# A two-layer hybrid encoder on one core: loads in turn, rotary angles beside the gated unit, first step sizes on GpSimd, one wait fewer at the recurrence

## The reference, cut to what matters

```python
proj = x @ w_in[i]
# recurrence: dt = exp(log_dt); lam_bar = exp(lam * dt); scan; gelu; gated unit
lam_bar = jnp.exp(lam * dt)
y = jax.nn.gelu(y.reshape(bsz, L, W_A))
y = y * jax.nn.sigmoid(y @ w_glu.astype(f32) + b_glu.astype(f32))
# attention: rotary angles of the positions, the same in both layers
ang = pos.astype(jnp.float32)[:, :, None, None] * inv
cos, sin = jnp.cos(ang), jnp.sin(ang)
...
mixed = jnp.sum(gates * lifted, axis=2) @ w_out[i]
x = layer_norm(DEEPNORM_ALPHA * x + mixed + ple, ln_g[i], ln_b[i])
```

## Time and profile before

| | us |
|---|---|
| median of three runs | 2646.0 |
| lowest, highest | 2645.92, 2646.96 |
| span of the profiled execution (first to last instruction) | 2645.0 |
| PE busy | 2577.1 |
| DVE busy | 1861.1 |
| ACT busy | 1288.8 |
| POOL busy | 111.0 |

### The profile page before, as it was taken

One profiled execution on the slowest core, in us unless ns is written; L12 is line 12 of the kernel. 1 busy time (PEld: TensorE's weight loads), 2 busy tenths in 40 slices (PEclk: granted clock), 3 DMA queues, 4 the chain that ended last, 5 costly groups with the idle time before them and its releaser, 6 DMA issues.

```text
span 2645.0 us, 41799 instructions
## 1 busy us (share of the span) xinstructions
PE 2577.1 (97%) x13736; PEld 2151.2 (81%) x13736; DVE 1861.1 (70%) x3251; ACT 1288.8 (49%) x2334; POOL 111.0 (4%) x206
## 2 busy tenths in 40 slices
PE   6999999999999999999989999999999999999998
PEld 5888999977777778898778999989767777788986
DVE  7788877834777776556678877887357777765666
ACT  5555555543444334443465555555334443444535
POOL 2100000000000000000021000000000000000000
PEclk9999999999999999999999999999999999999999
DMA  7544444434444335555464444444344444355454
GB/s 245 173 143 148 154 147 148 151 120 143 151 155 164 126 110 177 186 174 174 160 202 154 154 148 148 146 153 149 116 151 152 165 132 134 119 182 190 168 175 143
DMA packets 115956, 411.83 MB, mean 156 GB/s; under 512 B 15460, under 2 KB 15514, under 8 KB 115584
## 3 DMA queue, kind: packets, MB, share of 16 engines
q1 hardware_dynamic: 107424, 391.17, 43.9%
q0 software_dynamic: 8416, 19.18, 2.3%
HBM read 403.99 MB, written 6.29 MB: 155 GB/s over the span
## 4 chain that ended last, share of the span: by engine, by line
PE 93%; DVE 3%; issue 2%; ACT 2%; DMA 1%; PEldq 0%; PEld 0%; DVEq 0%; POOL 0%; POOLq 0%; ACTq 0%
PE bank L1623 29%; PE bank L1663 20%; PE bank L1665 10%; PE bank L2003 7%; PE bank L1580 5%; PE bank L1598 4%; PE bank L1753 2%; PE bank L1735 2%; PE bank L1923 2%; PE bank L1716 2%; PE bank L1937 1%; PE bank L1701 1%; PE bank L1821 1%; PE bank L1903 1%; PE bank L1845 1%
## 5 line engine op out<-in xcount | busy, mean ns | idle before, releaser
L384 ACT ACTIVATE WH<-ring 128x512 fp32r<-128x512 f32 x1364 | 854.8, 631 | 1136.5 <-PE bank L1623 473.0
L398 DVE TENSOR_TENSOR WL<-ring,WH 128x512 fp32r<-128x512 f32 x852 | 572.9, 688 | 417.6 <-ACT WH L384 415.2
L1663 PE MATMUL bank<-XX,WH 128*128 128x512 f32 x2304 | 823.7, 401 | 27.7 <-DVE XX L567 15.8
L1665 PE MATMUL bank<-XX,WL 128*128 128x256 f32 x2304 | 645.5, 280 | 0.0
L1663 PEld LDWEIGHTS bank<-XX,WH 128*128 128x128 f32 x2304 | 436.5, 189 | 130.1 <-DVE XX L567 15.8
L1623 PE MATMUL bank<-WH,XX 128*128 128x512 f32 x1536 | 485.2, 397 | 4.5 <-issue 3.5
L389 DVE TENSOR_TENSOR WL<-ring,WH 128x512 fp32r<-128x512 f32 x512 | 350.7, 688 | 140.1 <-ACT WH L384 135.9
L1665 PEld LDWEIGHTS bank<-XX,WL 128*128 128x128 f32 x2304 | 438.2, 190 | 0.0
L1623 PEld LDWEIGHTS bank<-WH,XX 128*128 128x128 f32 x1536 | 284.9, 188 | 81.4 <-issue 22.3
L1623 PE MATMUL bank<-WL,XX 128*128 128x512 f32 x768 | 299.9, 390 | 0.0
L1580 PE MATMUL bank<-ARENA,ring 128*128 128x256 f32 x704 | 158.3, 387 | 13.5 <-ACT ARENA L1368 11.0
(11 more groups left out here) (311 smaller groups left out, 3329.2 us busy)
## 6 DMA issues: line engine op xcount, KB each, us to landing
ring<-in_blocks SPq DMA_DIRECT2D x738, 512.0 KB, 3.3
ARENA<-in_bc POOLq DMA_DIRECT2D x2, 2048.0 KB, 8.9
ARENA<-in_decay POOLq DMA_DIRECT2D x8, 512.0 KB, 4.1
ARENA<-in_x SPq DMA_DIRECT2D x4, 512.0 KB, 9.3
u_scratch<-ARENA POOLq DMA_DIRECT2D x16, 128.0 KB, 2.4
ARENA<-u_scratch POOLq DMA_DIRECT2D x64, 32.0 KB, 3.1
y_scratch<-ARENA POOLq DMA_DIRECT2D x16, 128.0 KB, 2.0
ARENA<-y_scratch POOLq DMA_DIRECT2D x64, 32.0 KB, 2.7
```

Of the source, the lines that this page charges most:

```text
L384: nc.scalar.activation(wh[q], raw(which[0], q), ACT.Copy).then_inc(wh_ready[q], 1)
L398: vec.tensor_tensor(wl[q], raw(which[0], q), wh[q].bitcast(F32), ALU.subtract).then_inc(w_used[slot(which[0], half)], 1)
L1663: ins = mm(bank[b][:, :], h, xx[:, :, k, :], start=(k == 0), stop=(k == DT - 1), skip_group_check=True)
L1665: ins = mm(bank[b][:, 0:T], l, xh[:, k, :], start=False, stop=(k == DT - 1), skip_group_check=True)
```

## The change

1. SP issues w0, x0, x1, w1, x2, x3, w2, w3; ACT and DVE split w and x in the same turn, half by half.
2. The positions are no longer loaded at the start, but by POOL in each layer behind the last y loads. DVE makes the rotary phase in each layer behind the latent products, and ACT makes sin and cos in each layer behind its second Sqrt and ahead of the sigmoids of the gated unit. DVE no longer waits for `rope_ready` in the `ax` stage.
3. POOL makes the step sizes and angles of the first layer. Where DVE used one `scalar_tensor_tensor`, POOL uses two instructions (`mult_add`). The magnitude of the phase, S[8], is made by ACT (Abs) in both layers. The layer 1 values are still made by DVE in layer 0.
4. POOL issues LNP and BC behind the u loads of the second tile, no longer at the head of the layer.
5. PE no longer waits for both banks at the head of a turn of the recurrence.

The function bodies that are only moved are left out below.

```diff
--- before.py
+++ after.py
@@ -112,9 +112,9 @@
     "out":  [2, 2, 2, 2, 2, 2, 2, 2],
 }
 ZIN = 24 + 2
-DVE_STEPS, DVE_S5_STEPS = 437, 23
-SETUP_STEPS = 31
-ACT_STEPS, ACT_S5_STEPS = 8, 1
+DVE_STEPS, DVE_S5_STEPS = 445, 23
+SETUP_STEPS = 30
+ACT_STEPS, ACT_S5_STEPS = 9, 1
 PER_LAYER = [sum(FILLS[s][b] for s in STAGES) for b in range(8)]
@@ -249,6 +249,7 @@
         Y4 = area(0, 1)
         UP = [(ET if m < 4 else BK)[:, m % 4 * T:(m % 4 + 1) * T] for m in range(WT)]
         SP0 = area(25, 3)
+        TMP0 = area(28, 1)[:, 0:COLS]
         LRAW, GRAW = area(65, 3)[:, 0:640], area(68, 3)[:, 0:640]
         PA, PB = area(71, 1), area(72, 1)
@@ -263,6 +264,7 @@
         ROOTS = [area(117 + i, 1) for i in range(4)]
         PT = area(89, 4)
         KT, VV = area(93, 4), area(97, 8)
+        POS, ROPE_T = area(97, 1), [area(98 + i, 1) for i in range(4)]
         QN, QR, QT, KN = area(105, 8), area(113, 4), area(117, 4), area(121, 8)
         YC = area(51, 8)
@@ -309,7 +311,8 @@
         psum_full = [sem(f"psum_full{b}") for b in range(8)]
         psum_free = [sem(f"psum_free{b}") for b in range(8)]
         x_loaded = [sem(f"x_loaded{i}") for i in range(GROUPS)]
-        consts_loaded, pos_loaded, params_loaded, bc_loaded = sem("consts_loaded"), sem("pos_loaded"), sem("params_loaded"), sem("bc_loaded")
+        consts_loaded, pos_loaded, ang_loaded, params_loaded, bc_loaded = sem("consts_loaded"), sem("pos_loaded"), sem("ang_loaded"), sem("params_loaded"), sem("bc_loaded")
+        pool_step = sem("pool_step")
         setup_step, zeroed, b3_free = sem("setup_step"), sem("zeroed"), sem("b3_free")
         late_loaded = sem("late_loaded")
         b3_loaded, b3_cleared = sem("b3_loaded"), sem("b3_cleared")
@@ -404,8 +407,8 @@
             flat = blocks.rearrange("l b h p n -> (l b h) p n")
             for s in (0, 1):
                 sp.dma_start(slots[s], flat[s]).then_inc(w_loaded[s], 16)
-            for i in range(GROUPS):
-                sp.dma_start(group(RES, i), group(x, i)).then_inc(x_loaded[i], 16)
+                for i in (2 * s, 2 * s + 1):
+                    sp.dma_start(group(RES, i), group(x, i)).then_inc(x_loaded[i], 16)
             for s in (2, 3):
                 sp.dma_start(slots[s], flat[s]).then_inc(w_loaded[s], 16)
             with sp.Fori(1, DEPTH * HALVES // RING) as turn:
@@ -425,20 +428,86 @@
             sp.wait_ge(stored, GROUPS * 16)
+        def mult_add(v, st, out_, a, by, b):
+            if v is nc.gpsimd:
+                st.did(v.tensor_scalar(TMP0, a, by, None, ALU.mult)); st.wait()
+                st.did(v.tensor_tensor(out_, TMP0, b, ALU.add)); st.wait()
+            else:
+                st.did(v.scalar_tensor_tensor(out=out_, in0=a, scalar=by, in1=b, op0=ALU.mult, op1=ALU.add)); st.wait()
+        def round_phase(v, st, src, k, r, last=None):
+            st.did(v.tensor_scalar(k, src, INV_2PI, MAGIC, ALU.mult, ALU.add)); st.wait()
+            st.did(v.tensor_scalar(k, k, -MAGIC, None, ALU.add)); st.wait()
+            mult_add(v, st, r, k, -PI_1, src)
+            mult_add(v, st, r, k, -PI_2, r)
+            mult_add(v, st, r, k, -PI_3, r)
+            ins = v.tensor_scalar(r, r, PI_LOW, -PI_LOW, ALU.min, ALU.max)
+            if last is not None:
+                ins.then_inc(last, 1)
+            else:
+                st.did(ins); st.wait()
+        S = [SP0[:, i * COLS:(i + 1) * COLS] for i in range(12)]
+        lre, lim, ldt = (PAR[:, LP[name][0]:LP[name][1]] for name in ("lam_re", "lam_im", "log_dt"))
+        def step_sizes(v, sa):
...
+        def step_sizes_end(v, sa):
...
+        def step_angles(v, sa, angles_made):
+            dt, a, th = S[3], S[5], S[6]
+            sa.did(v.tensor_tensor(a, lre, dt, ALU.mult)); sa.wait()
+            sa.did(v.tensor_tensor(S[7], lim, dt, ALU.mult)); sa.wait()
+            round_phase(v, sa, S[7], S[0], th, half_angles)
+            sa.eng.wait_ge(half_angles, angles_made)
+            sa.did(v.tensor_scalar(TH, th, INV_2PI, None, ALU.mult)); sa.wait()
+            thd = TH.rearrange("p (c d q) -> p c d q", d=2, q=PAIRS)[:, :, 1, :]
+            sa.did(v.tensor_scalar(thd, thd, -1.0, None, ALU.mult))
+            sa.end()
         @block.gpsimd
         def _(pool):
             g = nc.gpsimd
-            pool.dma_start(U[:, 0:T].bitcast(I32), pos).then_inc(pos_loaded, 16)
-            pool.dma_start(ANG[:], angles).then_inc(pos_loaded, 16)
             pool.dma_start(PAR[:], lp[0]).then_inc(params_loaded, 16)
+            pool.dma_start(ANG[:], angles).then_inc(ang_loaded, 16)
+            pool.sem_inc(y4_free, 1)
+            sa = Steps(pool, pool_step, 0, SETUP_STEPS + 5)
+            pool.wait_ge(params_loaded, 16)
+            step_sizes(g, sa)
             pool.wait_ge(x_loaded[GROUPS - 1], 16)
             pool.dma_start(CON[:], consts).then_inc(consts_loaded, 16)
-            pool.sem_inc(y4_free, 1)
+            step_sizes_end(g, sa)
+            step_angles(g, sa, 1)
+            sa.wait()
+            pool.sem_inc(setup_step, SETUP_STEPS)
             with pool.Fori(0, DEPTH) as layer:
                 pool.wait_ge(xh_ready, layer * GROUPS + GROUPS)
                 pool.wait_ge(x_loaded[GROUPS - 1], 16)
-                pool.dma_start(LNP[:], ln[layer]).then_inc(bc_loaded, 16)
-                pool.dma_start(area(49, 16), bc[layer]).then_inc(bc_loaded, 16)
                 for m in range(WT):
@@ -449,6 +518,9 @@
                     by_step = u_scratch[layer, m].rearrange("(q g) (t c) -> t g q c", q=PAIRS, t=STEP)
                     for t in range(STEP):
                         pool.dma_start(split(U4[32 * t:32 * t + 32, m * T:(m + 1) * T], PAIRS), by_step[t]).then_inc(u4_loaded, 16)
+                    if m == 1:
+                        pool.dma_start(LNP[:], ln[layer]).then_inc(bc_loaded, 16)
+                        pool.dma_start(area(49, 16), bc[layer]).then_inc(bc_loaded, 16)
                 with pool.Fori(0, WT) as ct:
@@ -460,6 +532,7 @@
                     by_pair = y_scratch[ct].rearrange("(t g) (q c) -> q g t c", t=STEP, q=PAIRS)
                     for q in range(PAIRS):
                         pool.dma_start(split(U4[32 * q:32 * q + 32, bass.ds(ct * T, T)], STEP), by_pair[q]).then_inc(y_loaded, 16)
+                pool.dma_start(POS.bitcast(I32), pos).then_inc(pos_loaded, 16)
                 pool.wait_ge(yl_ready, layer * 4 + 1)
@@ -493,83 +566,16 @@
                 pool.wait_ge(late_loaded, layer * 64 + 64)
...
         @block.vector
         def _(dve):
             v = nc.vector
...
-            def step_angles(sa):
...
-                v.scalar_tensor_tensor(out=S[8], in0=th, scalar=-1.0, in1=th, op0=ALU.mult, op1=ALU.max).then_inc(half_angles, 1)
...
-            pre = Steps(dve, rope_arg, 0, 9)
-            dve.wait_ge(pos_loaded, 32)
-            pre.did(v.tensor_copy(U[:, T:2 * T], U[:, 0:T].bitcast(I32))); pre.wait()
-            pre.did(v.tensor_scalar(U[:, 2 * T:3 * T], U[:, T:2 * T], ANG[:, 0:1], None, ALU.mult)); pre.wait()
-            round_phase(dve, pre, U[:, 2 * T:3 * T], U[:, 3 * T:4 * T], U[:, 4 * T:5 * T])
-            r = U[:, 4 * T:5 * T]
-            pre.did(v.scalar_tensor_tensor(out=U[:, 5 * T:6 * T], in0=r, scalar=-1.0, in1=r, op0=ALU.mult, op1=ALU.max))
-            pre.end()
-            make_wl(dve, v, 0, B_AX)
-            for i in range(GROUPS):
-                dve.wait_ge(xh_ready, i + 1)
-                v.tensor_tensor(group(XL, i), group(RES, i), group(XH, i).bitcast(F32), ALU.subtract).then_inc(xl_ready, 1)
-            sa = Steps(dve, setup_step, 0, SETUP_STEPS)
-            dve.wait_ge(params_loaded, 16)
-            step_sizes(sa)
-            step_sizes_end(sa)
-            step_angles(sa)
+            for half in range(2):
+                make_wl(dve, v, 0, B_AX, halves=(half,))
+                for i in (2 * half, 2 * half + 1):
+                    dve.wait_ge(xh_ready, i + 1)
+                    v.tensor_tensor(group(XL, i), group(RES, i), group(XH, i).bitcast(F32), ALU.subtract).then_inc(xl_ready, 1)
             with dve.Fori(0, DEPTH) as layer:
                 st = Steps(dve, dve_step, layer, DVE_STEPS)
@@ -629,7 +635,6 @@
                 make_wl(dve, v, layer, B_AX + 4)
                 lr, li = ([LRAW[:, (r * 5 + k) * COLS:(r * 5 + k + 1) * COLS] for k in range(5)] for r in range(2))
-                dve.wait_ge(rope_ready, 1)
                 st.did(v.memset(lr[0], 1.0))
                 st.did(v.memset(li[0], 0.0))
                 st.did(v.tensor_scalar(lr[1], S[0], 1.0, None, ALU.add))
@@ -851,6 +856,13 @@
                         v.scalar_tensor_tensor(out=c, in0=c, scalar=par("kv_norm" if i else "q_norm", j), in1=rs,
                                                op0=ALU.mult, op1=ALU.mult).then_inc(latent_ready, 1)
+                dve.wait_ge(pos_loaded, layer * 16 + 16)
+                dve.wait_ge(ang_loaded, 16)
+                st.did(v.tensor_copy(ROPE_T[0], POS.bitcast(I32))); st.wait()
```

(40 more changed lines are left out.)

50 lines of the change are left out of this document (9 added, 41 removed).

## The result

The changed kernel takes 2677.93 us in the median of four runs (2675.78 to 2680.79), against 2646.48 (2645.92 to 2647.56) of the kernel before: a ratio of 1.012, 95% interval 1.0108 to 1.0133. It is slower, as forecast, and the time lies in the range, but the loss is 31.5 us where 15.7 were worked out.

The account below looks back on a forecast made before the run. PE, busy 97% of the span, was taken as the bound. 2645.0 (span) +23.0 -6.4 -2.7 +1.5 +0.3 = 2660.7, plus 1.0 from span to median: 2661.7, about 2662 us; range 2650 to 2680.

Parts of the forecast that it names:

- Part 1: Gated unit: the moved rotary chain delays ACT's sigmoid and so PE, 11.5 us a layer, 23.0 in all.
- Rival (d): Gated unit: rope_arg comes before the banks are full, so only extra load and Sin cost; 2643 or 2635, 8%.
- Part 2: Recurrence entry: removing PE's wait for both banks gains 3.2 us a layer, -6.4 in all.
- what is late next is the drain of PE's queue: Recurrence entry: after the removed wait only about 0.5 us of the 2.22 us stall remains, so 1.7 go.
- rival (b): Recurrence: the removed wait brings nothing, since the drain or the u stores are as late; +6.4, 2668, 10%.
- a cover of 7.6 us: Recurrence: time from the last u store's landing at 83.98 to PE's need of the result at 91.63.
- slow clock: PE behind a stall runs partly at 1.2 GHz: 1.5 us at the recurrence, 1.9 in gated unit and start.
- Part 4: Moved LNP and BC loads delay the u_scratch stores ACT awaits: 0 to 4 us a layer, 1.5 taken in all.
- Part 3: Start: PE begins at 8.5 to 10, block 2 at 30.1 behind POOL's steps of 0.5 us; gain 2.7 us.
- rival (a): Start: POOL's steps are dear (1.0 us each, 2679) or DVE and POOL exclude each other (2668); 18% for both.

Follow-up runs that it names:

- sin_late: Changed kernel with ACT's wait on rope_arg and its two Sin moved behind the fourth sigmoid of the gated unit: 2659.17 us, ratio 1.005.
- nowait_us4: Kernel before without PE's wait for both banks; ACT waits for four u stores ahead of turned, all eight only ahead of the copies: 2640.83 us, ratio 0.9978.
- only_nowait: Kernel before with only PE's wait for both banks at the recurrence taken out: 2646.55 us, ratio 0.9993.
- pool_late: Changed kernel with POOL's chain of steps held back until DVE has made WL of block 1: 2683.7 us in one run.

## Why the prediction was right or wrong

**Part 1, right.** +11.5 us a layer were forecast, 12.1 and 11.8 measured. The order of steps came as worked out: last latent product, a chain of 3.5 us (563.19 to 566.69), two Sin, table load, sigmoid. The table for Sin was loaded ahead of the wait (557.95), as assumed. sin_late takes the cost away by moving the wait in ACT's queue alone. Rival (d) fell: `rope_arg` came 9 us too late for it.

**Part 2, failed.** The step "what is late next is the drain of PE's queue" was right for PE's next matmul (0.61 us) and stopped there. It did not look at the next wait of ACT: ACT waits for all eight u stores ahead of `turned`, three blocks on, and when the last of them lands late, what was won is taken back. The forecast of 6.4 us was right for the wait (nowait_us4: 6.3) and wrong for the removal alone (only_nowait: 0 in the median, all of it in three of ten runs). It is what rival (b), at 10%, had said, with the u stores as one of its two reasons. The error was to reason the stores away with a cover of 7.6 us, taken from one trace and from a schedule in which PE was held back by the very wait that goes. The wait and its slow clock are 3.1 us of that cover (1.6 and 1.5); the landing, taken as fixed at 83.98, came 5.6 us later in the trace of only_nowait. In the kernel after, the sum of the same three gains (2.5 at the start, 1.6 of wait, 1.5 of slow clock) moves PE's demand from 91.63 to 85.99.

**Part 4, mis-sized.** I took 1.5 us in all. By the rows after: the store's landing comes from 83.98 to 91.05, 7.1 later; PE's demand 5.6 earlier; the cover was 7.6 less the 0.8 us that ACT needs from the landing until PE can go on (91.05 to 91.81). 7.1 + 5.6 - 6.8 = 5.9, and 5.8 and 5.9 are measured. Four slips add up: the 1.2 us of issue were named but not added to the delay (up to 6.3; it was 7.1, of which 5.4 are the third store's, 1.2 the issue and 0.5 the rest), the demand was put at 3 to 4 us earlier (5.6), ACT's part of the cover was forgotten, and the slow clock behind a wait was priced in every other part but not here. From my own bounds, a delay of 6.3 and a demand 4 earlier less 7.6, the answer would have been 2.7 us a layer and not 1.5 in all; the middle of "0 to 4" was a hope. What the slow clock cost follows from the stretch, as an estimate: 11.8 us longer, 11.7 of new waits, 3.2 of old wait and 3.0 of old slow clock gone, which leaves about 6.3 in all, 3.1 a layer. Parts 2 and 4 together: -4.9 forecast, +11.8 measured, 16.7 of the 18.5 us by which the spans' difference was missed. So these two are the steps that failed: a wait that was left out, and a term mis-sized at 1.5.

**Part 3, right in sum.** -2.7 forecast, -2.5 measured. PE starts at 8.89 (8.5 to 10), block 1 ends at 23.2 (23), block 2 starts at 31.67 (30.1). The price of a step was 0.42 us, below the 0.5 taken; alone the chain takes 15.1 us and not 17.6, that is 2.5 us to the good. Against it stand 5.1 us of steps held up by DVE (20.2 less 15.1), the one half of rival (a) that held. With PAR 0.8 us earlier (7.21, not 8) and 4.3 for 4.5 us behind the chain, that gives the 1.6 us by which block 2 came late. It so started 3.05 us earlier than before, not 4.6; but of that only 0.6 was lost by the end of `ax`, where 1.9 had been put down, since behind the wait the block takes 7.2 us for 5.7, 1.5 lost, and the 0.7 us stall of before at 40.4 is gone. Two errors of more than 1 us each cancelled, which is luck. The Trainium skill's page "SBUF — State Buffer" (SBUF: two separate sides) says that a DVE operation with two SBUF inputs and a GpSimd instruction that reads SBUF block each other for the whole instruction; pool_late agrees, with 0.37 us alone against 1.08 and 1.32 beside DVE. Its price, 5.1 us, is near the 6 that rival (a) had put on it (12 operations at 0.5 us); block 2 came earlier than its 36 for the other three reasons.

**The range** held by luck, because its upper end had been set for another cause, rival (a) with 1.0 us a step. Parts 2 and 4 had bounds of their own, at least -3.4 and at most 4 us a layer, so +4.6 together at the worst; +11.8 was measured.

## What to carry to other kernels

When a wait goes, the next one to look at is not only on the same engine: list every wait that the following stages make for transfers, and measure its cover against the new, earlier demand and against the latest landing that the traces show, not one of them. A merged wait ("all eight have landed") costs as much as its last part; split it to where each part is needed. An in-order engine that frees the banks of another must not be given a wait ahead of doing so: behind the fourth sigmoid the same instructions cost almost nothing.
